# Layer-norm statistics of a diffusion block: full-width TensorE sums, or four narrow products side by side

## The chip, the cores and the metric

The kernel runs on one core of one Trainium2 chip. The metric is device time in microseconds (us) of one execution; lower is better. A core has a matrix engine (TensorE, PE in the profile, with its weight loads as PEld), three engines for elementwise work (VectorE or DVE, ScalarE or ACT, GpSimd or POOL) and queues for transfers. SBUF is the on-chip memory that holds tiles of 128 partitions. PSUM is the memory into which TensorE writes; its banks hold 512 float32 columns on each partition. A matmul with stationary weights of K x M and a moving tile of K x N gives M partitions by N columns, and its time goes by N.

## The reference

Two layers of a hybrid block work on 512 latent tokens and 256 context tokens of width 1024. Each layer is half FFN, token mixing, half FFN, and behind each of the three stands a layer-norm over the 1024 features of a token:

```
def layernorm(x, g, b):
    mu = jnp.mean(xf, axis=-1, keepdims=True)
    var = jnp.mean(jnp.square(xf - mu), axis=-1, keepdims=True)
    return ((xf - mu) * lax.rsqrt(var + LN_EPS) * g + b)

def half_ffn(x, shift, scale, gate, w_in, w_out, g, b):
    h = modulate(x, shift, scale)              # x * (1 + scale) + shift
    a, u = jnp.split(h @ w_in, 2, axis=-1)
    y = (jax.nn.silu(a) * u) @ w_out
    return layernorm(ALPHA * x + 0.5 * gate * y, g, b)
```

The mixers are a Hyena and a gated recurrence in layer 0 and a latent attention in layer 1. The context is carried through layer 0 and the first half FFN of layer 1 only; the output is the latent stream.

## The kernel before

**Layout.** X holds the residual stream with features on partitions: X[128, chunk, token], eight chunks (KC) of 128 features and 768 tokens (TOK), the 512 latents (LAT) first and then the 256 of context (CTX). A layer-norm thus has to add over partitions and over the eight chunks. The program numbers its layer-norms ln0 to ln4 and "final". ln0 to ln3 are worked in two parts: a=0 the context, a=1 the latents. ln4 and final have only latents, in two halves of 256.

**Large products.** Every float32 product of weights and activations is split into high and low parts in the format fp32r, and made of three products: high by high, high by low, low by high (the three lines of `product`, 2914 to 2916, and of `columns`, 2960 to 2962). HHI and HLO are the high and low part of the modulated activations h; GHIA, GLOA, GHIB, GLOB those of the gated ones; WHI*, WLO* those of the weights.

**The statistics.** GpSimd adds some chunks of X into RSTD ahead of TensorE (`add_chunks`, line 844; the table X_ADDED says how many chunks are folded: 7 of the context, 4 of the latents). TensorE then adds what is left over chunks and partitions: `sums` (line 2925) multiplies by ONES, a 128x128 matrix of ones, in plain float32, so that each of the 128 output partitions holds the same sum. ScalarE scales it to the mean MU (line 1292), VectorE subtracts it from X (`center`, line 1842), ScalarE squares (line 1297, tiles SQ), TensorE adds the squares in the same way (`variance`, line 2936), ScalarE takes the root into RSTD (line 1302), VectorE the reciprocal of the whole tile (`inverse`, line 1848) and multiplies (`norm`, line 1855). Mean and root thus stand in SBUF on all partitions, 256 or 512 columns wide. Behind `norm`, ScalarE makes h and its high part (lines 1054, 1057) and VectorE its low part (`low`, line 1825), chunk by chunk; TensorE waits for each chunk of it (semaphore h_lo).

**What sets the order.** Each engine has one hand-written instruction stream, held together by counting semaphores; nothing is scheduled by a planner. TensorE works strictly in its order. Around a layer-norm of two parts it runs: the down products of the context, eight down products of the latents of which the first is followed by the context's sums and the fifth by its variance, then the latents' sums; then `first_pair`, the first products of the next layer: context columns of output half 0 of the slots A and B, the latents' variance, context columns of half 1, and the latent columns. While TensorE makes the context columns of half 1, the latents' root, reciprocal and norm go on beside it. The down product of a chunk of 512 latents is six products of 512 columns; a step k of context columns is three products of 256 columns for each slot. VectorE adds each down product to X (`last_chunk`, line 2272, "eviction" below). ln1 is spread in the same way over the output products of the even mixer, ln4 over those of the odd mixer; in final, the second half's sums and both variances follow the last down product, and then the transposes for the output (line 3659).

**An existing form with narrow weights.** The products of the conditioning vectors (`ada_products`, line 2821) use 32 stationary columns each, four products side by side into the four strips of 32 output partitions.

Of the kernel before, what the change touches and what calls it, by code (L numbers as in the profile page):

```python
# [17 lines left out]
P = 128  # L18
D = 1024
# [9 lines left out]
X_ADDED = {1: 7, 0: 4}  # L29
# [118 lines left out]
def build(nc, A, out):  # L148
# [32 lines left out]
    MU = sb("MU", [P, TOK])  # L181
# [132 lines left out]
    for t, name in ((WQH, "WQH1"), (WQL, "WQL1")):  # L314
# [40 lines left out]
    ln_add, ln_sum, ln_var, ln_mu, ln_cen, ln_sq, ln_std, ln_rstd, ln_n, ln_h32, ln_x = (  # L355
        sem(f"ln_{n}") for n in ("add", "sum", "var", "mu", "cen", "sq", "std", "rstd", "n", "h32", "x"))
# [228 lines left out]
    STAT_BANKS = {"ln0": (3, 4), "ln1": (7, 6), "ln2": (3, 4), "ln3": (3, 4), "ln4": (6, 7), "final": (0, 1)}  # L585
# [6 lines left out]
    def stat_bank(name, a):  # L592
        _, n, s = part(name, a)
        return PS[STAT_BANKS[name][a if name in HALVED else s]][:, 0:n]

# [403 lines left out]
    def _(act):  # L999
# [286 lines left out]
        def layernorm(name, S, j, nxt):  # L1286
            p = plan[name]

            def mean(a):
                lo, n, _ = part(name, a)  # L1290
# [8 lines left out]
            def root(a):  # L1299
                lo, n, _ = part(name, a)  # L1300
                act.wait_ge(ln_var, p.ln + a + 1)
                act.activation(RSTD[:, lo:lo + n], stat_bank(name, a), ACT.Sqrt, bias=EPS[:, 0:1],
                               scale=1.0 / D).then_inc(ln_std, 1)

            if name == "final":
# [5 lines left out]
                mean(1)  # L1311
                for m in range(KC):
                    if m == KC // 2:
                        root(0)
                    square(1, m)
# [362 lines left out]
    def _(dve):  # L1678
# [158 lines left out]
        def center(name, S, a, m):  # L1837

            lo, n, _ = part(name, a)
            if m == 0:  # L1840
                dve.wait_ge(ln_mu, plan[name].ln + a + 1)
            dve.tensor_tensor(X[:, m, lo:lo + n], X[:, m, lo:lo + n], MU[:, lo:lo + n], ALU.subtract).then_inc(ln_cen, 1)

        def inverse(name, S, a):

            lo, n, _ = part(name, a)
            dve.wait_ge(ln_std, plan[name].ln + a + 1)
            dve.reciprocal(RSTD[:, lo:lo + n], RSTD[:, lo:lo + n]).then_inc(ln_rstd, 1)
            dve.wait_ge(ln_rstd, plan[name].ln + a + 1)
            dve.wait_ge(ln_sq, KC * (plan[name].ln + a + 1))  # L1850

        def norm(name, S, a, m):

            lo, n, _ = part(name, a)
            dve.tensor_tensor(X[:, m, lo:lo + n], X[:, m, lo:lo + n], RSTD[:, lo:lo + n], ALU.mult).then_inc(ln_n, 1)
# [36 lines left out]
        def ffn(name, S, j, ada, t0, then, nxt, tables=None):  # L1892
# [86 lines left out]
            if S == 1:  # L1979
# [6 lines left out]
                for m in range(KC):  # L1986
                    center(then, 1, 0, m)
                    if m + 3 < KC:
                        half_chunk(1, m + 3)
                for m in range(KC):  # L1990
# [800 lines left out]
        for a in range(2):  # L2791
            inverse("final", 1, a)
            lo, n, _ = part("final", a)
# [895 lines left out]
```

## Time and profile before

| | |
|---|---|
| time, three runs | 2953.30, 2946.63, 2952.29 us; median 2952.29 us |
| span of the profiled execution | 2945.3 us |
| PE busy | 2859.7 us, 97% of the span, 16175 products |
| PEld busy | 2469.8 us, 84% |
| DVE busy | 2030.9 us, 69% |
| ACT busy | 1049.0 us, 36% |
| POOL busy | 295.6 us, 10% |
| PE waiting in `first_pair` for the low part of h (L2960 <- DVE HLO L1825) | 8.6 us in 5 waits, the longest 4.3 us |
| PE waiting for GpSimd's pre-added chunks (L2925 <- POOL RSTD L844) | 3.3 us in 3 waits |

The span is the time from the first to the last instruction in the profiled execution; the median of the three timed runs is 7.0 us above it, which is what lies around the span and how far a run differs from another. In the profile, a product in plain float32 leaves two records, since it makes two passes; an fp32r product leaves one. Products overlap their neighbours, so what a product costs is read from the distance between starts, not from its own duration. The granted clock (PEclk) is 9 tenths or more in all forty slices of the page, but it can fall in short stretches. In this span ln0 lies at about 645 to 705 us, ln1 at 985 to 1045, ln2 at 1578 to 1640, ln3 at 2119 to 2185, ln4 at 2505 to 2577 and final at 2895 to 2945.

### The profile page before, as it was taken

The numbers are of one execution on the slowest core, as the hardware profiler recorded it, in microseconds if no ns is written. First come the engines' busy times: TensorE is split into PE (matmuls) and PEld (weight loads), VectorE is DVE, ScalarE is ACT, GpSimd is POOL, SyncE is SP. The second block draws the span as 40 slices with busy tenths as digits, with TensorE's granted clock in tenths as the row PEclk, the third lists the DMA queues.
The fourth block names the chain that finished last, engine by engine and source line by source line (L and its number), as shares of the span: only waits on it lengthen the run. The fifth ranks groups of instructions, "written<-read, shape, count | busy, mean of one in ns | idle before, by whom it ended". The sixth has DMA issues, their size and how long they took to land.

```text
span 2945.3 us, 44152 instructions
## 1 busy us (share of the span) xinstructions
PE 2859.7 (97%) x16175; PEld 2469.8 (84%) x16175; DVE 2030.9 (69%) x3254; ACT 1049.0 (36%) x1651; POOL 295.6 (10%) x403
## 2 busy tenths in 40 slices
PE   6999999999999999999999999999999999999998
PEld 2688999987875878998988899999877998878887
DVE  4467767776767477677776887777776887654545
ACT  1422223325650342232323433333255665422123
POOL 1000000011100100101001000000103654100000
PEclk9999999999999999999999999999999999999999
DMA  7434432221213233534432122222310101233331
GB/s 287 147 132 150 144 126 65 64 72 46 61 59 114 86 100 118 174 123 161 129 95 58 43 65 74 69 71 64 88 48 20 29 21 44 58 115 100 100 100 43
DMA packets 301696, 269.64 MB, mean 92 GB/s; under 512 B 31175, under 2 KB 257327, under 8 KB 301456
## 3 DMA queue, kind: packets, MB, share of 16 engines
q1 hardware_dynamic: 278960, 188.95, 21.7%
q0 software_dynamic: 21760, 76.03, 7.3%
q10 hardware_dynamic: 864, 3.15, 0.3%
q8 instruction: 72, 1.18, 0.2%
q14 instruction: 40, 0.33, 0.0%
HBM read 262.85 MB, written 5.24 MB: 91 GB/s over the span
## 4 chain that ended last, share of the span: by engine, by line
PE 88%; DVE 6%; DMA 2%; ACT 2%; issue 1%; POOL 1%; SPq 0%; POOLq 0%; DVEq 0%; ACTq 0%
PE PSALL L2914 14%; PE PSALL L2915 14%; PE PSALL L2916 14%; PE PSALL L3169 8%; PE PSALL L3170 8%; PE PSALL L3171 8%; PE PSALL L2821 2%; PE PSALL L2936 2%; PE PSALL L2960 2%; PE PSALL L2961 2%; PE PSALL L2962 2%; PE PSALL L3592 1%; PE PSALL L3577 1%; PE PSALL L2863 1%; DMA RAW<-in_ffn_w_in_dram 1%
## 5 line engine op out<-in xcount | busy, mean ns | idle before, releaser
L2048 DVE SCALAR_TENSOR_TENSOR X<-PSALL,GATE,X 128x512 f32<-128x512 f32 x480 | 279.5, 611 | 99.7 <-PE PSALL L2916 99.1
L3169 PE MATMUL PSALL<-HHI,WSH 128*128 128x384 f32 x816 | 274.1, 336 | 5.8 <-DVE HLO L2246 5.8
L3170 PE MATMUL PSALL<-HLO,WSH 128*128 128x384 f32 x816 | 274.2, 336 | 0.0
L3171 PE MATMUL PSALL<-HHI,WSL 128*128 128x384 f32 x816 | 273.5, 335 | 0.0
L2914 PE MATMUL PSALL<-GHIA,WHIW 128*128 128x512 f32 (+1 forms) x618 | 217.2, 351 | 13.2 <-DVE X L2048 10.2
L2915 PE MATMUL PSALL<-GLOA,WHIW 128*128 128x512 f32 (+1 forms) x618 | 212.9, 344 | 0.0
L2916 PE MATMUL PSALL<-GHIA,WLOW 128*128 128x512 f32 (+1 forms) x618 | 212.3, 344 | 0.0
L2916 PE MATMUL PSALL<-GHIB,WLOW 128*128 128x512 f32 (+1 forms) x618 | 212.2, 343 | 0.0
L2915 PE MATMUL PSALL<-GLOB,WHIW 128*128 128x512 f32 (+1 forms) x618 | 212.1, 343 | 0.0
L2914 PE MATMUL PSALL<-GHIB,WHIW 128*128 128x512 f32 (+1 forms) x618 | 212.0, 343 | 0.0
L1174 ACT ACTIVATE WSH<-RAW 128x512 fp32r<-128x512 f32 x204 | 129.0, 632 | 223.0 <-DVE RAW L2125 151.3
L3169 PE MATMUL PSALL<-TH,WSH 128*128 128x384 f32 x612 | 206.6, 338 | 0.0
L3171 PE MATMUL PSALL<-TH,WSL 128*128 128x384 f32 x612 | 205.2, 335 | 0.0
L3170 PE MATMUL PSALL<-TL,WSH 128*128 128x384 f32 x612 | 204.7, 334 | 0.0
L2914 PE MATMUL PSALL<-HHI,WHIA 128*128 128x512 f32 (+1 forms) x464 | 168.8, 364 | 1.5 <-DVE WLOA L1724 1.5
L2916 PE MATMUL PSALL<-HHI,WLOA 128*128 128x512 f32 (+1 forms) x464 | 165.3, 356 | 0.0
L2915 PE MATMUL PSALL<-HLO,WHIA 128*128 128x512 f32 (+1 forms) x464 | 165.3, 356 | 0.0
L1065 ACT ACTIVATE WHIW<-RAW 128x1024 fp32r<-128x1024 f32 x96 | 100.0, 1054 | 178.5 <-PE PSALL L2916 97.5
L3169 PEld LDWEIGHTS PSALL<-HHI,WSH 128*128 128x128 f32 x816 | 154.0, 189 | 6.7 <-issue 6.7
L828 POOL DMA_DIRECT2D ADA<-in_ada_w_dram x144 | 76.1, 529 | 824.8 <-PE PSALL L2821 734.0
L2914 PE MATMUL PSALL<-HHI,WHIB 128*128 128x512 f32 (+1 forms) x432 | 157.5, 365 | 1.3 <-DVE MOD L1714 1.3
L844 POOL TENSOR_TENSOR RSTD<-X 128x256 f32<-128x256 f32 (+1 forms) x12 | 14.2, 1184 | 1416.6 <-DVE X L2272 871.2
(411 smaller groups left out, 7329.0 us busy)
## 6 DMA issues: line engine op xcount, KB each, us to landing
RAW<-in_ffn_w_in_dram SPq DMA_DIRECT2D x176, 512.0 KB, 4.1
ADA<-in_ada_w_dram POOLq DMA_DIRECT2D x144, 512.0 KB, 5.6
RAW<-in_ffn_w_out_dram SPq DMA_DIRECT2D x88, 512.0 KB, 3.9
RAW<-in_ev_w_in_dram SPq DMA_DIRECT2D x20, 512.0 KB, 4.0
WRAW<-in_mla_w_q_up_dram SPq DMA_DIRECT2D x16, 288.0 KB, 3.0
RAW<-in_ev_w_out_dram SPq DMA_DIRECT2D x8, 512.0 KB, 4.5
RAW<-in_mla_w_in_dram SPq DMA_DIRECT2D x8, 512.0 KB, 4.3
RAW<-in_mla_w_out_dram SPq DMA_DIRECT2D x8, 512.0 KB, 3.8
```

Source lines behind the costliest of these rows:

```text
L828: pool.dma_start(ADA[slot][:, :], src).then_inc(ada_in[slot], 16)
L1065: act.activation(WHI[slot][:, 1024 * half:1024 * half + 1024], RAW[raw_slot(q)][:, :], ACT.Copy).then_inc(hi_done, 1)
L1174: return act.activation(WSH[:, place, :], raw[:, 512 * cols:512 * cols + 512], ACT.Copy)
L2048: dve.scalar_tensor_tensor(X[:, m, lo:lo + n], down_bank(m, s, 2), GATE[:, j, m, s:s + 1], X[:, m, lo:lo + n], ALU.mult, ALU.add).then_inc ...
L2821: x = te.matmul(PS[3][32 * j:32 * j + 32, 0:D // 4], SC[:, k, :], ADA[slot][:, j * D // 4:(j + 1) * D // 4], start=(k == 0), stop=(k == KC ...
L2914: te.matmul(out, w_hi, x_hi(k), start=(k == 0), stop=False)
L2915: te.matmul(out, w_hi, x_lo(k), start=False, stop=False)
L2916: x = te.matmul(out, w_lo, x_hi(k), start=False, stop=(k == ks - 1))
L2936: x = te.matmul(stat_bank(name, a), ONES[:, :], squares_at(name, a, m), start=(m == 0), stop=(m == KC - 1))
L3169: te.matmul(out, w_hi, hi[block](k), start=(k == 0), stop=False)
L3170: te.matmul(out, w_hi, low[block](k), start=False, stop=False)
L3171: x = te.matmul(out, w_lo, hi[block](k), start=False, stop=(k == 3))
```

## The change

The sums and the squares of a layer-norm are no longer made by one product with 128 columns of ones. `column_sums` makes four products with 32 columns of ones, each on a quarter of the tokens, into the four strips of 32 partitions of one bank. The result is compact: 64 columns (of 256 tokens) or 128 columns (of 512), and the token's quarter is its strip. Mean (MUC), root and reciprocal (RSC) are taken on these compact tiles. `spread` then brings them to all partitions: four products, each with one column of the identity, repeated over 128 weight columns, as weights, and the compact tile as moving data; they write a full-width PSUM bank, from which `center`, `norm` and the last scaling of final now read their second operand, in place of MU and RSTD in SBUF. TensorE has a mean spread and a root spread for each of the twelve parts, with new waits (ln_mu and ln_rstd), and VectorE waits for the spreads (ln_mean, ln_root). GpSimd folds 5 chunks of the context, no longer 7, and TensorE two more.

The pieces are placed anew. In the down products of the latents, the mean is spread after chunk 1, the context's variance comes after chunk 5 instead of 4, and the root is spread after chunk 6. In `first_pair` the latent mean is spread between steps 0 and 1 of the context columns of half 0, the latents' variance lies in four pieces of two chunks each behind steps 0 to 3 of half 1, and the root is spread behind all columns of half 1. ln1, ln4 and final have their own places, as in the diff. ScalarE takes final's first root ahead of the second half's squares, and VectorE its reciprocal between the two centrings.

By count, 28 products of 256 columns and 20 of 512 in `sums`, and 64 and 32 in `variance`, become 100 groups of four products of 64 columns and 52 groups of four of 128; added are 24 spreads of four products, 16 of them 64 columns wide and 8 of 128. The groups stand in 39 separate runs between products of the ordinary form.

```diff
-X_ADDED = {1: 7, 0: 4}
+X_ADDED = {1: 5, 0: 4}
...
-    STAT_BANKS = {"ln0": (3, 4), "ln1": (7, 6), "ln2": (3, 4), "ln3": (3, 4), "ln4": (6, 7), "final": (0, 1)}
+    SUM_BANKS = {"ln0": (4, 6), "ln1": (6, 6), "ln2": (4, 6), "ln3": (4, 6), "ln4": (6, 6), "final": (3, 1)}
+    WIDE_BANKS = {"ln0": (3, 7), "ln1": (7, 3), "ln2": (3, 7), "ln3": (3, 7), "ln4": (7, 5), "final": (4, 0)}
...
-                act.activation(MU[:, lo:lo + n], stat_bank(name, a), ACT.Copy, scale=1.0 / D).then_inc(ln_mu, 1)
+                act.activation(compact(MUC, name, a), sum_bank(name, a), ACT.Copy, scale=1.0 / D).then_inc(ln_mu, 1)
...
-                act.activation(RSTD[:, lo:lo + n], stat_bank(name, a), ACT.Sqrt, bias=EPS[:, 0:1],
+                act.activation(compact(RSC, name, a), sum_bank(name, a), ACT.Sqrt, bias=EPS[:, 0:1],
...
-                dve.wait_ge(ln_mu, plan[name].ln + a + 1)
-            dve.tensor_tensor(X[:, m, lo:lo + n], X[:, m, lo:lo + n], MU[:, lo:lo + n], ALU.subtract).then_inc(ln_cen, 1)
+                dve.wait_ge(ln_mean, plan[name].ln + a + 1)
+            dve.tensor_tensor(X[:, m, lo:lo + n], X[:, m, lo:lo + n], wide_bank(name, a), ALU.subtract).then_inc(ln_cen, 1)
...
-            dve.reciprocal(RSTD[:, lo:lo + n], RSTD[:, lo:lo + n]).then_inc(ln_rstd, 1)
+            dve.reciprocal(compact(RSC, name, a), compact(RSC, name, a)).then_inc(ln_rstd, 1)
...
+            if m == 0:
+                dve.wait_ge(ln_root, plan[name].ln + a + 1)
+                dve.wait_ge(ln_sq, KC * (plan[name].ln + a + 1))
+            dve.tensor_tensor(X[:, m, lo:lo + n], X[:, m, lo:lo + n], wide_bank(name, a), ALU.mult).then_inc(ln_n, 1)
...
+        def column_sums(name, a, m, src):
+            w = quarter(name, a)
+            for q in range(4):
+                x = te.matmul(sum_bank(name, a)[32 * q:32 * q + 32, :], ONES[:, 0:32], src[:, w * q:w * q + w],
+                              start=(m == 0), stop=(m == KC - 1))
+            return x
+        def spread(name, a, t):
+            w = quarter(name, a)
+            for q in range(4):
+                x = te.matmul(wide_bank(name, a)[:, w * q:w * q + w], ID[:, 32 * q:32 * q + 1].broadcast_to([P, P]),
+                              compact(t, name, a), start=True, stop=True)
+            return x
...
-                columns(0, [(slot, 0) for slot in "AB"])
-                variance(ln, 2, 1)
-                columns(0, [(slot, 1) for slot in "AB" if halves[slot] > 1])
+                columns(0, [(slot, 0) for slot in "AB"], lambda k: mean_out(ln, 1) if k == 0 else None)
+                columns(0, [(slot, 1) for slot in "AB" if halves[slot] > 1],
+                        lambda k: variance(ln, 2, 1, (2 * k, 2 * k + 1)) if k < 4 else None)
+                root_out(ln, 1)
...
                     sums(then, 1, 1, lambda m: e0 + KC + m + 1)
+                    variance(then, 1, 0)
+                    mean_out(then, 1)
+                    root_out(then, 0)
+                    variance(then, 1, 1)
+                    root_out(then, 1)
...
                     if m == 0:
                         sums(then, 2, 0, lambda m: e0 + m + 1)
-                    if m == 4:
+                    if m == 1:
+                        mean_out(then, 0)
+                    if m == 5:
                         variance(then, 2, 0)
+                    if m == 6:
+                        root_out(then, 0)
...
-            unit_product("ev_out", "W", p.q + 6, 0, 0, order).then_inc(pe["W"], 1)
+            unit_product("ev_out", "W", p.q + 6, 0, 0, order, after=lambda k: root_out("ln1", 0) if k == 3 else None).then_inc(pe["W"], 1)
...
             chunk(4, 1, between=lambda: sums("ln4", 2, 0, evicted(0)))
+            mean_out("ln4", 0)
...
-            chunk(7, 1)
+            chunk(7, 1, between=lambda: root_out("ln4", 0))
```

**Place 1: TensorE, down products of the latents ahead of ln2, from the end of chunk 0 to the start of chunk 2.** RSTD holds GpSimd's sum of chunks, evac counts evictions. Before:

```order
L2925 MATMUL PSALL<-RSTD,ONES 128x256 [waits ln_add]
L2925 MATMUL PSALL<-X,ONES 128x256 [waits evac]
L2914 MATMUL PSALL<-GHIA,WHIW 128x512
L2915 MATMUL PSALL<-GLOA,WHIW 128x512
L2916 MATMUL PSALL<-GHIA,WLOW 128x512
L2914 MATMUL PSALL<-GHIB,WHIW 128x512
L2915 MATMUL PSALL<-GLOB,WHIW 128x512
L2916 MATMUL PSALL<-GHIB,WLOW 128x512
L2914 MATMUL PSALL<-GHIA,WHIW 128x512 [waits evac]
```

After:

```order
L2950 MATMUL PSALL<-X,ONES 32x64 [waits evac]
L2950 MATMUL PSALL<-X,ONES 32x64 x3
L2929 MATMUL PSALL<-GHIA,WHIW 128x512
L2930 MATMUL PSALL<-GLOA,WHIW 128x512
L2931 MATMUL PSALL<-GHIA,WLOW 128x512
L2929 MATMUL PSALL<-GHIB,WHIW 128x512
L2930 MATMUL PSALL<-GLOB,WHIW 128x512
L2931 MATMUL PSALL<-GHIB,WLOW 128x512
L2958 MATMUL PSALL<-MUC,ID 128x64 [waits ln_mu]
L2958 MATMUL PSALL<-MUC,ID 128x64 x3
L2929 MATMUL PSALL<-GHIA,WHIW 128x512 [waits evac]
```

Two full products of the sums have become four groups of four narrow ones (the last of them is shown), and the spread of the mean, with its wait for ScalarE, stands behind chunk 1.

**Place 2: TensorE, `first_pair` of ln3, where the context columns pass from half 0 to half 1.** SQ are the latents' squares; slot B has one output half of 64 columns here, slot A has two of 128. Before:

```order
L2961 MATMUL PSALL<-HLO,WHIB 64x256
L2962 MATMUL PSALL<-HHI,WLOB 64x256
L2936 MATMUL PSALL<-SQ,ONES 128x512 [waits ln_sq,ln_mu]
L2936 MATMUL PSALL<-SQ,ONES 128x512 [waits ln_sq] x7
L2960 MATMUL PSALL<-HHI,WHIA 128x256 [waits lo_done,h_lo]
L2961 MATMUL PSALL<-HLO,WHIA 128x256
L2962 MATMUL PSALL<-HHI,WLOA 128x256
L2960 MATMUL PSALL<-HHI,WHIA 128x256 [waits h_lo]
```

After:

```order
L3005 MATMUL PSALL<-HHI,WLOB 64x256
L3003 MATMUL PSALL<-HHI,WHIA 128x256 [waits lo_done,h_lo]
L3004 MATMUL PSALL<-HLO,WHIA 128x256
L3005 MATMUL PSALL<-HHI,WLOA 128x256
L2950 MATMUL PSALL<-SQ,ONES 32x128 [waits ln_sq]
L2950 MATMUL PSALL<-SQ,ONES 32x128 x3
L2950 MATMUL PSALL<-SQ,ONES 32x128 [waits ln_sq]
L2950 MATMUL PSALL<-SQ,ONES 32x128 x3
L3003 MATMUL PSALL<-HHI,WHIA 128x256 [waits h_lo]
L3004 MATMUL PSALL<-HLO,WHIA 128x256
```

The variance, one block of eight full products ahead of half 1, is now cut into four pieces inside it.

**Place 3: TensorE, `first_pair` of ln3, where the context columns end and the latent columns (512 wide) begin.** RSC is the compact reciprocal root. After:

```order
L3003 MATMUL PSALL<-HHI,WHIA 128x256 [waits h_lo]
L3004 MATMUL PSALL<-HLO,WHIA 128x256
L3005 MATMUL PSALL<-HHI,WLOA 128x256
L2958 MATMUL PSALL<-RSC,ID 128x128 [waits ln_rstd]
L2958 MATMUL PSALL<-RSC,ID 128x128 x3
L3003 MATMUL PSALL<-HHI,WHIA 128x512 [waits h_lo]
```

Before, the three rows of the last context step were followed at once by the latent columns; now the spread of the root, with its wait for VectorE's reciprocal, stands between them. In ln0, ln2 and ln4 it stands at the same place.

## Rows read from the trace of the kernel before

**Rows 1.** Groups by form, TensorE, line 2936: busy us, mean ns | idle.

```profile
L2936 PE MATMUL PSALL<-SQ,ONES 128*128 128x256 f32 x128 | 28.8, 379 | 0.0
L2936 PE MATMUL PSALL<-SQ,ONES 128*128 128x512 f32 x64 | 28.1, 592 | 0.0
```

**Rows 2.** Timeline, TensorE: start us, us, operation, xcount [idle before <-releaser].

```profile
1071.91 0.39 PE L2916 MATMUL PSALL<-HHI,WLOA 128*128 128x512 f32 x1
1072.23 1.93 PE L2821 MATMUL PSALL<-ADA,SC 128*32 128x256 f32 x32
...
1074.32 0.28 PE L2915 MATMUL PSALL<-HLO,WHIA 128*128 128x256 f32 x1
```

**Rows 3.** Timeline, TensorE, first products of line 2821.

```profile
36.53 0.42 PE L2821 MATMUL PSALL<-ADA,SC 128*32 128x256 f32 x4 [0.98 <-issue]
```

**Rows 4.** Timeline, TensorE, products of 128 columns in the up projections.

```profile
1566.31 0.27 PE L3132 MATMUL PSALL<-TL,WHIB 128*128 128x128 f32 x1
1566.42 0.28 PE L3133 MATMUL PSALL<-TH,WLOB 128*128 128x128 f32 x1
```

**Rows 5.** Groups by form, VectorE (out<-in as partitions x elements) and ScalarE.

```profile
L1848 DVE RECIPROCAL RSTD<-RSTD 128x256 f32<-128x256 f32 x8 | 14.0, 1748 | 5.5 <-ACT RSTD L1302 5.5
L1848 DVE RECIPROCAL RSTD<-RSTD 128x512 f32<-128x512 f32 x4 | 13.4, 3353 | 25.2 <-ACT RSTD L1302 25.2
L1302 ACT ACTIVATE RSTD<-PSALL,EPS 128x512 f32<-128x512 f32 x4 | 2.8, 689 | 19.6 <-PE PSALL L2936 19.6
```

**Rows 6.** Timeline, VectorE and GpSimd, centring of ln2's context.

```profile
1589.09 2.52 DVE L1842 TENSOR_TENSOR X<-X,MU 128x256 f32<-128x256 f32 x4
...
1589.25 1.40 POOL L844 TENSOR_TENSOR RSTD<-X 128x512 f32<-128x512 f32 x1 [3.81 <-DVE X L2272]
```

**Rows 7.** Timeline, ln2, TensorE and VectorE.

```profile
1585.50 0.70 PE L2925 MATMUL PSALL<-RSTD,ONES 128*128 128x256 f32 x2 [1.09 <-POOL RSTD L844]
...
1598.63 1.09 DVE L1855 TENSOR_TENSOR X<-X,RSTD 128x256 f32<-128x256 f32 x3
...
1603.67 0.68 PE L2960 MATMUL PSALL<-HHI,WHIA 128*128 128x256 f32 x1
...
1620.99 1.29 DVE L1855 TENSOR_TENSOR X<-X,RSTD 128x512 f32<-128x512 f32 x2
...
1623.97 0.50 PE L2960 MATMUL PSALL<-HHI,WHIA 128*128 128x512 f32 x1 [1.39 <-DVE HLO L1825]
```

**Rows 8.** Timeline, ln3: last eviction, first context column, first latent column.

```profile
2144.47 0.74 DVE L2272 SCALAR_TENSOR_TENSOR X<-PSALL,GATE,X 128x512 f32<-128x512 f32 x1
...
2146.30 0.68 PE L2960 MATMUL PSALL<-HHI,WHIA 128*128 128x256 f32 x1
...
2166.48 0.80 PE L2960 MATMUL PSALL<-HHI,WHIA 128*128 128x512 f32 x1 [4.26 <-DVE HLO L1825]
```

**Rows 9.** Windows behind three TensorE waits: us, PE busy (x), PEclk, DMA share, GB/s.

```profile
1711.60:1715.00 3.40, 3.40 (x13) 0.50 0.02 5
2166.50:2172.40 5.90, 5.90 (x14) 0.50 0.00 0
2596.30:2599.00 2.70, 2.70 (x12) 1.00 0.59 194
```

**Rows 10.** Timeline, ln4: second mean and norm, and a TensorE wait after it.

```profile
2549.63 0.37 ACT L1292 ACTIVATE MU<-PSALL 128x256 f32<-128x256 f32 x1
...
2560.09 0.76 DVE L1855 TENSOR_TENSOR X<-X,RSTD 128x256 f32<-128x256 f32 x2
...
2576.94 0.50 PE L2914 MATMUL PSALL<-HHI,WHIA 128*128 128x512 f32 x1 [1.48 <-DVE WLOA L1724]
```

**Rows 11.** Timeline, VectorE, final layer-norm, second half of the tokens.

```profile
2934.14 3.25 DVE L2796 SCALAR_TENSOR_TENSOR X<-X,VECS,RSTD 128x256 f32<-128x256 f32 x8
```

**Rows 12.** Timeline, TensorE, products behind its other long waits.

```profile
1710.15 0.41 PE L3169 MATMUL PSALL<-HHI,WSH 128*128 128x384 f32 x1 [3.31 <-DVE HLO L2246]
...
2596.30 0.50 PE L2914 MATMUL PSALL<-GHIA,WHIW 128*128 128x512 f32 x1 [2.59 <-DVE X L1927]
```

More of the change, by code:

```diff
@@ L354, in build @@
     evac = sem("evac")
-    ln_add, ln_sum, ln_var, ln_mu, ln_cen, ln_sq, ln_std, ln_rstd, ln_n, ln_h32, ln_x = (
-        sem(f"ln_{n}") for n in ("add", "sum", "var", "mu", "cen", "sq", "std", "rstd", "n", "h32", "x"))
+    ln_add, ln_sum, ln_var, ln_mu, ln_mean, ln_cen, ln_sq, ln_std, ln_rstd, ln_root, ln_n, ln_h32, ln_x = (
+        sem(f"ln_{n}") for n in ("add", "sum", "var", "mu", "mean", "cen", "sq", "std", "rstd", "root", "n", "h32", "x"))
     flt_in, tab_in, kf_out = sem("flt_in"), sem("tab_in"), [sem(f"kf_out{n}") for n in range(2)]
@@ L1311, in layernorm @@
                 mean(1)
+                root(0)
                 for m in range(KC):
-                    if m == KC // 2:
-                        root(0)
                     square(1, m)
@@ L1989, in ffn @@
                         half_chunk(1, m + 3)
+                inverse(then, 1, 0)
                 for m in range(KC):
@@ L2946, in first_pair, with columns @@
                            for t in (WHI, WLO)]
-            def columns(a, outs):
+            def columns(a, outs, after=None):
                 lo, n, s = part(ln, a)
@@ L2952, in columns @@
                 for k in range(KC):
+                    if after and k:
+                        after(k - 1)
                     te.wait_ge(h_lo, h + KC * a + k + 1)
@@ L3282, in wide, with unit_product @@
                     sums(then, 2, 0, lambda m: e0 + m + 1)
-                if m == 4:
+                if m == 1:
+                    mean_out(then, 0)
+                if m == 5:
                     variance(then, 2, 0)
+                if m == 6:
+                    root_out(then, 0)
             sums(then, 2, 1, lambda m: e0 + KC + m + 1)
-        def unit_product(name, slot, lo_at, half, s, order, wait=None, heads=None):
+        def unit_product(name, slot, lo_at, half, s, order, wait=None, heads=None, after=None):
             lo, width = SEGS[s]
@@ L3298, in unit_product @@
                            lambda k: moving(0, order[k]), lambda k: moving(1, order[k]),
-                           (lambda k: wait(order[k], s)) if wait else None)
+                           (lambda k: wait(order[k], s)) if wait else (lambda k: after(k - 1)) if after else None)
         def gates(n, s):
@@ L3651, in _ @@
         ffn("ffn3", 1, 0, "ln4", "final")
-        variance("final", 1, 0)
-        variance("final", 1, 1)
         for e, (t, half) in enumerate(FIN_TILES):
```

52 lines of the change are left out of this document (32 added, 20 removed).

## The prediction

> **What bounds the kernel now.** I read the page first. TensorE is busy for 97% of the span (the table above). So two things can move the time: less work on TensorE, and the stretches in which it waits for another engine. Next the groups by form: a float32 product with 128 columns of ones costs 28.8/64 = 0.45 us at 256 columns and 28.1/32 = 0.88 us at 512, both passes counted [rows 1]. The 28 + 64 products of 256 and 20 + 32 of 512 are thus 41.4 + 45.8 = 87 us of TensorE. Then the timeline of each layer-norm: TensorE waits 1.09 us for GpSimd ahead of ln2's context sums and 1.39 us for the low part of h ahead of its latent columns [rows 7], 4.26 us at that place in ln3 [rows 8]. ln0 has ln2's shape. Last the clock: behind the 4.26 us wait the granted clock was 0.50, that is 1.2 GHz, for the next 5.9 us [rows 9].
>
> **What the new operations cost.** No row shows a 32-wide product of 64 or 128 columns, so I go by the nearest.
> - *Side by side.* Line 2821 makes 16 products of 256 columns in 1.93 us from first start to last end [rows 2], where one alone takes 0.45; four run at once. A group of four then costs a quarter of a full product: 0.11 us (64 columns each) or 0.22 (128). From above: if every pass costs what it costs in line 2821, 1.72/32 = 0.054 us, a group of eight passes costs 0.43 whatever its width.
> - *Entering and leaving the form.* From 1071.91 to 1074.32 is 2.41 us [rows 2]. In it lie one product of 512 (half of 5.9/14, so 0.21, [rows 9]), sixteen of line 2821 (four groups of 0.43) and one of 256 (0.12). About 0.35 is left for both changes of form. With 39 runs that is 13.7 us.
> - *A spread.* Its weights are 128 columns wide, and with such weights two products of 128 columns start 0.11 us apart [rows 4]. Four products of two passes make 8 x 0.11 = 0.88 us, and 0.17 until the last has landed. From below 0.45 (256 columns at full rate), from above double, 1.8, should loading a repeated column be slower.
> - *VectorE, ScalarE.* The reciprocal takes 1.75 us at 256 and 3.35 at 512 columns [rows 5], 0.0063 a column and 0.14 fixed: 0.54 at 64, 0.95 at 128. A root of 512 takes 0.69 [rows 5]; for 128 I take 0.35. An eviction that reads PSUM lasts 0.74 at 512 columns [rows 8], norm's two from SBUF 1.29, with the last one's tail [rows 7]: a PSUM operand costs between nothing and 0.1 a chunk; I take nothing.
> - *Contention.* Four centrings of 256 took 2.52 us while GpSimd added a chunk [rows 6]; three norms of the same form take 1.09 alone [rows 7], so four take 1.43. 1.1 us went to GpSimd. Centre now has a PSUM operand, and I expect the loss gone; if not, the context's norm comes 1.1 later.
>
> In TensorE work: 100 x 0.11 + 52 x 0.22 = 22, switches 14, spreads 24 x 0.88 = 21, together 57 against 87: 30 us less. But most of what goes stood where VectorE and ScalarE needed the time, so I follow each stage.
>
> The Trainium skill, TensorEngine Tiling (Array Packing), Key Properties, says that changing the tiling mode drains TensorE. The trace agrees, with the 0.35 us above; without a drain the result would be better by up to 14 us.
>
> **ln2, and ln0 like it: 1.7 us each.** Context: with fewer chunks folded the GpSimd wait of 1.09 goes. Sums: 4 groups 0.43 + 0.35; the mean spread is 1.05; the variance 0.86 + 0.35 for 3.6. The context's root comes one down chunk later, VectorE's reciprocal is 1.2 shorter and contention 1.1 less, but the root must pass TensorE behind chunk 6 (0.88 and two handovers). Norm starts at about 1597.7 where it was 1598.63. The last eviction, which the latents' sums need, moves with it, and the last sum behind it takes 0.22, not 0.88: the first context column comes at about 1602.5 instead of 1603.67. From there to the first latent column it took 20.3 us (1623.97). Now: 96 products of 0.12 = 11.5; mean spread 1.05; four variance pieces of 2 x 0.22 + 0.35 = 3.1; root and reciprocal 1.6, covered by the four steps (2.9) behind the last piece; root spread 1.05; then norm, h, its high and its low part, 1620.99 to 1623.97 = 3.0 before and nothing beside it now. Sum 19.7. Gain 0.6 + 1.1.
>
> **ln3: 4.9 us and 2.7 us of clock.** The context's norm comes 1.2 earlier by the same steps, so the last eviction ends at about 1 us before 2145.2 and the first context column is at 2144.3, not 2146.30 [rows 8]: 2.0. From there it took 20.2. Now 72 x 0.12 = 8.6, mean 1.05, pieces 3.1, root and reciprocal 1.6 of which 1.1 are covered, root spread 1.05, then 3.0: 17.3. Gain 2.9. The stretch at half clock held 14 products in 5.9 us [rows 9], which at 0.23 are 3.2: 2.7 more, if the clock stays.
>
> **ln1: 0.7 us.** Its context is bound by VectorE and ScalarE; only the shorter latent reciprocal shows, less the spread.
>
> **ln4: 3.8 us lost.** The latent mean of the second half is made on ScalarE behind five chunks of h, at 2549.63 [rows 10]. The spread of it stands on TensorE behind the first step of columns, queued ahead of seven steps that did not need it. They start at about 2550.4 instead of 2547.4. From there 7 x 0.72, half 1's 8 x 0.72, four pieces of 2 x 0.11 + 0.35 and the root spread, which now stands behind all of half 1: 2550.4 + 5.0 + 5.8 + 2.3 + 0.9 = 2564.4, less up to 0.5 for ScalarE's shorter root and mean ahead of it. Norm was at 2560.09, with half 1 beside it. VectorE's chain behind it is tight up to WLOA, for which TensorE already waits at 2576.94, so the loss passes through.
>
> **final: 2.0 us.** The second scaling starts at 2934.14 [rows 11] and sets the end. Variances of 8 groups cost 1.2, not 3.6, and the two reciprocals 1.2 less each; the second half's mean and root spreads and the root's handovers take back 3. I get about 2932.1.
>
> **Clock.** In ln0, ln2, ln3 and ln4 nothing covers norm and h behind the root spread, so TensorE waits about 3.1 us. Two other waits of before were 3.31 us, ended by the product at 1710.15, and 2.59, ended at 2596.30 [rows 12]; the granted clock was 0.50 from 1711.6 behind the first and 1.00 behind the second [rows 9]. 3.1 lies between. A half clock costs some 1.4 us, half of what ln3 paid for its longer wait. I charge two of four: 2.8.
>
> **Sum.** 1.7 + 1.7 + 0.7 + 4.9 + 2.7 - 3.8 + 2.0 - 2.8 = 7.1 us. On the profiled span that is 2945.3 - 7.1 = 2938.2; with the 7.0 us by which the median exceeds the span, 2945.2 us.
>
> **Rivals.**
> - *Full saving (0.08).* TensorE is the bound to the end, 97% busy, and 26 to 30 us less of its work come through: 2927 at best, or 2935 where only ln4's loss and the clock fail to appear. Against it: at each latent norm the chain through VectorE is what counts.
> - *Given back (0.27).* The clock falls behind all four waits and stays down for longer (another 3 to 6 us), or a start has a price of its own. If eight starts take 0.2 us where the columns need 0.11, the 100 groups of 64 columns cost 9 us more, of which about half lies on the path: 2950. The row of four products as one stretch of 0.42 us [rows 3] shows them beside each other, but doesn't show the starts of passes a quarter as long. Either way 2949 to 2953. The Trainium skill, TensorE: Matmul & The Clock Gate, section "Wait — 56ns, not 53.3ns?", puts the least distance of two starts at about 25 ns, whatever the width; by that the eight passes take 0.2 us, and it is this rival's second form. No run here shows it yet.
> - *The loads set the pace (0.20).* A pass of 64 columns is too short to hide the load of its weights. At 0.054 us a pass a group costs 0.43: 100 x 0.32 + 52 x 0.21 = 43 us more, three quarters of it on the path: 2977. With only the spreads at twice the price, 21 us more, some 19 of 24 on the path: 2962. It decides once a group costs 0.06 us more on average, or a spread 1.3 us. For it speaks that products of 128 columns stand 0.11 apart [rows 4], twice what their columns take; against it that line 2821 kept 0.054 a pass with a load for each, and may be faster still.
> - The forecast's own case has 0.45; its own range is 2937 to 2950.
>
> **How the numbers follow.** Changes under 0.2%, 5.9 us, can't be told from none. Faster: 0.08, most of the forecast case (0.38 of 0.45), and a little of the second rival (0.04): 0.50. Same: the other 0.07, and 0.23 of that rival: 0.30. Slower: 0.20. The range 2934 to 2960 leaves out half of the first rival and most of the third.
>
> **What would show it.** In the profile after: groups of L2950 at 0.11 or 0.22 us, a spread (L2958) at 0.9; ln2's first latent column about 20 us behind its first context column; ln3's about 17, with the clock at 1.00 behind it; ln4's second norm 3.8 later against the last context eviction; TensorE waits of 3.1 us ahead of four latent stretches. The prediction is wrong if L2950's groups are dearer than 0.2 us, if a spread takes over 1.3, or if ln4's first columns are not held by the mean's spread.

## The result, and the profile after

The changed kernel is slower: 2958.70 us (median of ten, 2954.01 to 2964.19) against 2952.23 us (median of ten), ratio 1.0026, 95% interval 1.0017 to 1.0035. Forecast were 2945.2 us. The sign was wrong. The measured time lies inside the stated range, 2934 to 2960, but no case of the text that has this mechanism ends there.

The two profiled executions lie apart by more, 15.3 us (spans 2945.3 and 2960.6): that of before was a low one (2946.63 us) and that of after a high one (2962.55). So I don't compare spans but stages. VectorE runs the same 3254 instructions in both kernels, nearly all in the same order; the difference of the start of the same instruction in two profiles, taken ahead of and behind a layer-norm, tells what that stage gained or lost, whatever went on elsewhere. Positive is later than before. In times of before the stages run from 640 to 740, 985 to 1100, 1575 to 1690, 2110 to 2240, 2500 to 2620 and 2895 to 2938 us; another choice of the instruction moves a number by 0.3 us or less, in final by up to 0.5.

| stage | forecast, without the clock | after | second profile of after |
|---|---|---|---|
| ln0 | -1.7 | +0.9 | +0.9 |
| ln1 | -0.7 | +3.4 | +3.3 |
| ln2 | -1.7 | +2.2 | -1.7 |
| ln3 | -7.6 | -5.4 | -5.3 |
| ln4 | +3.8 | +8.6 | +8.2 |
| final | -2.0 | -1.6 | -1.6 |
| sum | -9.9 | +8.1 | +3.8 |
| outside these stages | 0 | +6.8 | +6.2 |

What lies outside comes in a few single jumps of 0.4 to 2.6 us at the program's start, in ada loads and in other half-clock stretches, at other places in each profile.

The new operations first, groups by form of the changed kernel:

```profile
L2950 PE MATMUL PSALL<-SQ,ONES 128*32 128x64 f32 x512 | 11.3, 223 | 0.1
L2950 PE MATMUL PSALL<-SQ,ONES 128*32 128x128 f32 x256 | 10.3, 279 | 0.0
L2958 PE MATMUL PSALL<-MUC,ID 128*128 128x128 f32 x32 | 7.3, 408 | 0.0
L2958 PE MATMUL PSALL<-RSC,ID 128*128 128x128 f32 x32 | 4.3, 278 | 0.0
```

The variances of 64 squares of 256 and 32 of 512 columns took 28.8 and 28.1 us [rows 1]; they take 11.3 and 10.3, changes of form included. And two groups of the same shape, the spreads of four means and of four roots of 512 tokens, differ: 7.3 and 4.3 us. Equal work at unequal cost is a matter of the clock, as the windows below show. The timeline of ln2's context variance, in plain products, shows the unit prices:

```profile
1601.22 0.39 PE L2931 MATMUL PSALL<-GHIB,WLOW 128*128 128x512 f32 x1
1601.54 1.10 PE L2950 MATMUL PSALL<-SQ,ONES 128*32 128x64 f32 x64
1602.57 0.50 PE L2929 MATMUL PSALL<-GHIA,WHIW 128*128 128x512 f32 x1
1602.90 0.40 PE L2930 MATMUL PSALL<-GLOA,WHIW 128*128 128x512 f32 x1
```

The sixty-four passes (two of each product) start within 0.88 us, 14 ns apart on average: eight groups of 0.11. Another 0.15 pass until the next ordinary product starts. With 0.09 more than usual at the entrance and 0.10 more behind, a change in and out costs 0.34. The forecast had 0.11 and 0.35. VectorE's part:

```profile
L1866 DVE TENSOR_TENSOR X<-X,PSALL 128x512 f32<-128x512 f32 x32 | 21.5, 681 | 9.0 <-PE PSALL L2958 9.0
L1858 DVE RECIPROCAL RSC<-RSC 128x64 f32<-128x64 f32 x8 | 4.4, 546 | 9.7 <-ACT RSC L1314 9.7
L1858 DVE RECIPROCAL RSC<-RSC 128x128 f32<-128x128 f32 x4 | 3.8, 954 | 24.1 <-ACT RSC L1314 24.1
```

Reciprocals of 0.55 and 0.95, as in the sum, for 1.75 and 3.35 [rows 5]. The contention is gone too: beside a GpSimd add of 1.29 us, four centrings with a PSUM operand take 1.41, where they took 2.52 [rows 6]:

```profile
1598.11 1.41 DVE L1853 TENSOR_TENSOR X<-X,PSALL 128x256 f32<-128x256 f32 x4
1598.27 1.29 POOL L858 TENSOR_TENSOR RSTD<-X 128x512 f32<-128x512 f32 x1 [5.93 <-DVE X L2284]
```

So every operation is as cheap as it was priced. Now TensorE in ln2, in the changed kernel's timeline, where [rows 7] had two waits:

```profile
1605.39 1.10 PE L2958 MATMUL PSALL<-RSC,ID 128*128 128x64 f32 x8 [1.17 <-DVE RSC L1858]
...
1609.66 0.43 PE L2950 MATMUL PSALL<-X,ONES 128*32 128x128 f32 x8 [0.90 <-DVE X L2284]
1610.99 0.66 PE L2950 MATMUL PSALL<-X,ONES 128*32 128x128 f32 x8 [0.90 <-DVE X L2284]
1613.02 1.74 PE L2958 MATMUL PSALL<-MUC,ID 128*128 128x128 f32 x8
...
1628.42 1.05 PE L2958 MATMUL PSALL<-RSC,ID 128*128 128x128 f32 x8
1632.48 0.79 PE L3003 MATMUL PSALL<-HHI,WHIA 128*128 128x512 f32 x1 [3.02 <-DVE HLO L1836]
```

Before, full products of 0.88 us filled the time until VectorE had evicted the next chunk; the groups of 0.22 don't, and TensorE waits 1.17, 0.90 and 0.90 us within seven microseconds. Behind that the mean's spread takes 1.74 us where the root's takes 1.05. And the latent columns begin behind a wait of 3.02. ln0 is like it; in ln3 the sums have only the two waits of 0.90, the first of them here:

```profile
2154.54 0.42 PE L2950 MATMUL PSALL<-X,ONES 128*32 128x128 f32 x8 [0.90 <-DVE X L2284]
```

The windows of the changed kernel in ln2 (us, PE busy (x), PEclk, DMA share, GB/s) name the cause:

```profile
1609.00:1611.00 2.00, 0.44 (x10) 1.00 0.00 0
1611.00:1614.40 3.40, 3.40 (x21) 0.50 0.00 0
1613.00:1614.50 1.50, 1.50 (x10) 0.52 0.00 0
1614.40:1616.40 2.00, 2.00 (x19) 0.99 0.01 4
1631.50:1638.30 6.80, 5.82 (x14) 0.50 0.00 0
1632.45:1638.50 6.05, 6.02 (x15) 0.51 0.00 0
```

The granted clock is half at both places, 1.2 GHz. The run before had one such stretch in ln0 to ln4 [rows 9]; this one has twelve, each 3.4 or 6.8 us long, 51 us together: in each of the five layer-norms at its first columns (behind the thin sums) and at its latent columns (behind the wait for h), and two more about ln4.

The other runs say the same. Each has its mean granted clock on record: a run at 0.985 over 2957 us spent 0.030 of them, 89 us, at half clock. By this it is 90 us on average in the ten runs of the change (77 to 101), 55 us in the 29 runs of before that stand beside the first experiments. Over all 132 runs on record, compared with runs of the same kernel in the same series, each further microsecond of half clock goes with 0.33 us more time. The 35 us more are then some 12 us, an estimate, against the 6.5 us by which the change is slower.

### The profile page after: what moved, and what is told of

The parts are those of the page before. It is cut to its first block, busy times and chain, and to the rows that moved or that the text cites. A ratio compares the mean times of both kernels' runs of the same rounds, so it can differ in the third digit from the quotient of the medians.

```text
span 2960.6 us, 46366 instructions
## 1 busy us (share of the span) xinstructions
PE 2857.2 (97%) x17295; PEld 2481.4 (84%) x17295; DVE 2009.5 (68%) x3254; ACT 1043.2 (35%) x1651; POOL 287.4 (10%) x395
## 3 DMA queue, kind: packets, MB, share of 16 engines
q8 instruction: 81, 1.33, 0.2%
## 4 chain that ended last, share of the span: by engine, by line
PE 88%; DVE 6%; DMA 2%; ACT 1%; issue 1%; SPq 0%; POOL 0%; DVEq 0%; ACTq 0%; POOLq 0%
PE PSALL L2929 14%; PE PSALL L2930 14%; PE PSALL L2931 14%; PE PSALL L3224 8%; PE PSALL L3225 8%; PE PSALL L3226 8%; PE PSALL L3003 2%; PE PSALL L3005 2%; PE PSALL L3004 2%; PE PSALL L2836 2%; PE PSALL L3652 2%; PE PSALL L3637 1%; PE PSALL L2878 1%; PE PSALL L3517 1%; PE PSALL L2958 1%
## 5 line engine op out<-in xcount | busy, mean ns | idle before, releaser
L2930 PE MATMUL PSALL<-HLO,WHIB 128*128 128x512 f32 (+1 forms) x432 | 154.6, 358 | 0.0
```

The lines of the kernel that those rows point to most:

```text
L2930: te.matmul(out, w_hi, x_lo(k), start=False, stop=False)
```

## The same program twice

The changed kernel was profiled a second time to see whether the stretches belong to their places.

> The changed kernel unchanged, for a second profile of it. If the half-clock stretches belong to the places, the same ten stand at the same places in ln0 to ln4. If they are a matter of chance at places that allow them, some are gone and others have come, and the ledger of ln0 and ln2 moves between -1.7 us (none) and +2 (two or three), 1.75 us for each stretch of 3.5 us.

Measured: 2957.5 us. In ln2 the same waits, to a hundredth, and another clock. (This profile was taken with a later series, perhaps on another chip: which chip made the first one is not on record. But the ten runs of the change in one series differ among themselves by up to 24 us of half clock.) Timeline of TensorE in ln2, second profile:

```profile
1610.40 0.43 PE L2950 MATMUL PSALL<-X,ONES 128*32 128x128 f32 x8 [0.90 <-DVE X L2284]
1611.72 0.43 PE L2950 MATMUL PSALL<-X,ONES 128*32 128x128 f32 x8 [0.90 <-DVE X L2284]
1612.89 1.05 PE L2958 MATMUL PSALL<-MUC,ID 128*128 128x128 f32 x8
...
1631.66 0.50 PE L3003 MATMUL PSALL<-HHI,WHIA 128*128 128x512 f32 x1 [3.01 <-DVE HLO L1836]
```

and its windows:

```profile
1612.80:1614.00 1.20, 1.20 (x13) 1.00 0.00 0
1632.35:1638.50 6.15, 6.15 (x28) 1.00 0.00 0
```

In 6.1 us behind the wait it starts 28 products, the first profile 15. ln2 comes out at -1.7 us, the forecast's own number for it without a fall; with 10.2 us of half clock it was +2.2. That is 3.9/10.2, or 0.38 us lost for each microsecond of half clock (it would be 0.50 if TensorE had work all through; part lies in waits), near the 0.33 of the runs. ln0, ln1 and ln3 kept their stretches; in ln4 there are again four, but one stands elsewhere and one is only half as long. The second profile has ten, 38 us together. The first latent column of ln2 follows the first context column by 19.6 us here, where the forecast had 19.7. The expectation named "ten"; I had not counted two of ln4's. The Trainium skill, TensorE: Matmul & The Clock Gate, section "What's actually happening", says of a kernel's first products that the point at which the clock changes differs from run to run of one kernel; here that is so in the middle of a kernel, with 3.9 us between the two profiles in one stage.

## The experiments

### Filling the waits ahead of the latent columns

```diff
                 root_out(ln, 1)
+                for i in range(12):
+                    te.matmul(PS[6][:, 0:P], ONES[:, :], ID[:, :], start=True, stop=True)
```

> The changed kernel with twelve extra float32 products of 128 columns (about 0.22 us each at full clock, so 2.6 us) behind the root spread of ln0 to ln4, in the wait of 2.5 to 3.2 us ahead of the latent columns; their result is used by nothing. Clock theory (the idle waits pull the granted clock to 0.50 for the first 3 to 4 us of the latent columns): the clock stays at 1.00 behind the filler, the columns start when they did, and each of the five places gains 1.2 to 2.4 us, 7 to 9 us in all, so about 2950. Order theory (the loss is the wait itself, the clock is a side effect): the columns start no earlier, the time is within 2 us of the changed kernel's 2958.7. Price theory (the new small products are dearer than they look): 13 us of more products, later by up to that.

Measured: 2953.20 us, ratio to before 1.0006 (0.9996 to 1.0017), 5.5 us faster than the change. None of the five latent stretches is at half clock any more, where without filling 27 of 35 were (five layer-norms in each of the seven profiles that have the root spread in its place of the change); those at the first columns remain in ln1, ln3 and ln4. ln0 and ln2 stand at -1.7, ln1 at +0.7. The columns start no earlier: what comes of it comes by the clock. TensorE's timeline in ln2 shows 0.34 us of wait left of 3.02:

```profile
1632.39 0.50 PE L3003 MATMUL PSALL<-HHI,WHIA 128*128 128x512 f32 x1 [0.34 <-DVE HLO L1836]
1632.73 0.40 PE L3004 MATMUL PSALL<-HLO,WHIA 128*128 128x512 f32 x1
```

It brought 5.5 where 7 to 9 were expected. The mean half clock of its runs is 70 us, 20 fewer than the change has, and at 0.33 that is 6.6. That ln0 and ln2 lost the stretches at their first columns too, where nothing was filled, is chance.

### Filling the gaps in the latents' sums

```diff
             for m in [0] + list(range(count + 1, KC)) if ms is None else ms:
+                if a == 1 and m >= 6 and name in ("ln0", "ln2", "ln3"):
+                    for i in range(3):
+                        te.matmul(PS[4][:, CTX:CTX + P], ONES[:, :], ID[:, :], start=True, stop=True)
                 te.wait_ge(*((ln_add, done + count) if m == 0 else (evac, evicted(m))))
```

> The changed kernel with three extra float32 products of 128 columns (0.22 us each) ahead of each of the last two groups of the latents' sums in ln0, ln2 and ln3, where TensorE waits 0.9 us twice for evictions; their result is used by nothing. Clock theory (TensorE, thinly used around the narrow sums, falls to half clock for the next 3 us): the clock stays at 1.00 at the first context columns and the mean spread, each of the three gains 1.0 to 1.5 us, 2955. If what the chip sees is the narrow products themselves and not the gaps, the clock falls all the same and the time is the changed kernel's, 2958.7 to 2960.

Measured: 2954.34 us, ratio 1.0009 (0.9997 to 1.0021), 4.4 us faster than the change. In ln0, ln2 and ln3, which were filled, no stretch stands at the first columns; in ln1 and ln4, which were not, it does. In the nine profiles in which these gaps are not filled, 15 of 27 first columns of the three layer-norms ran at half clock; in this one and the last one below, where the gaps are filled, none of six. With the narrow products unchanged, it is the gaps between them that let the clock fall. In ln3, which has no wait of 1.17, two of 0.90 us are enough.

### The late mean of ln4

```diff
-                columns(0, [(slot, 0) for slot in "AB"], lambda k: mean_out(ln, 1) if k == 0 else None)
+                columns(0, [(slot, 0) for slot in "AB"], lambda k: mean_out(ln, 1) if k == (4 if ln == "ln4" else 0) else None)
```

> The changed kernel with the spread of ln4's second mean behind step 4 of the context columns, not behind step 0. Order theory: TensorE no longer stands 2.4 us for ScalarE's mean, so ln4's second norm comes 2.4 us earlier. Clock theory: the half-clock stretch behind that wait (6.5 us, 3.2 lost) goes as well, so 5 to 5.6 us in all, 2953.5. If the spread's place does not matter (the squares would hold the variance anyway): no change, 2958.7.

Measured: 2956.93 us (2949.62 to 2965.62), ratio 1.0024 (1.0013 to 1.0035). The median moved by 1.8 us, within what the runs scatter. In the profile ln4 stands at +4.8, not +8.6, but it has 10 us less of half clock there, which has its part in the 3.9. In the changed kernel the spread waited 2.44 us for ScalarE and ran at half clock:

```profile
2557.88 1.97 PE L2958 MATMUL PSALL<-MUC,ID 128*128 128x64 f32 x8 [2.44 <-ACT MUC L1305]
```

in this one there is no wait:

```profile
2550.13 1.00 PE L2958 MATMUL PSALL<-MUC,ID 128*128 128x64 f32 x8
```

To part the two, the distance from ln4's first root spread to its second: 24.01 us in the change with 6.8 us of half clock between, 23.07 in the run with filled waits with 3.4, and 20.10 here with none. That is 0.28 us for a microsecond of half clock, and some 2.0 us for the place of the spread, near the 2.4 expected. In its ln0 and ln2, where nothing was changed, no clock fell, and they stand at -1.7 both: the same chance as above.

### The root spread beside the last steps

```diff
-                columns(0, [(slot, 1) for slot in "AB" if halves[slot] > 1],
-                        lambda k: variance(ln, 2, 1, (2 * k, 2 * k + 1)) if k < 4 else None)
-                root_out(ln, 1)
+                late = 3 if halves["B"] > 1 else 5
+                columns(0, [(slot, 1) for slot in "AB" if halves[slot] > 1],
+                        lambda k: variance(ln, 2, 1) if k == 0 else root_out(ln, 1) if k == late else None)
```

> The changed kernel with the latents' variance in one piece behind step 0 of the context columns of half 1, and the root spread behind step 3 (step 5 in ln3) and not behind all eight. Order theory: norm and h then run beside the last four steps (2.9 us), the wait of about 3 us ahead of the latent columns goes nearly whole in ln0, ln1, ln2 and ln4, a third of it in ln3, and three switches of form fewer give 1 us each: about 3 to 4 us for each of the four and 1.5 in ln3, 14 us, so about 2945; with the clock kept on top another 5, so 2940. Clock theory alone: without the wait the clock stays up, gain 1.5 us a place, 2951. Price theory: 3 us of switches saved, 2956.

Measured: 2935.70 us, ratio 0.9955 (0.9940 to 0.9970), 23.0 us faster than the change and 16.5 faster than before. The forecast of this run, 14 to 19, was too small. TensorE in ln2 has no wait behind the spread:

```profile
1613.81 1.05 PE L2958 MATMUL PSALL<-RSC,ID 128*128 128x128 f32 x8
...
1617.88 0.50 PE L3003 MATMUL PSALL<-HHI,WHIA 128*128 128x512 f32 x1
```

4.07 us from spread to latent columns as in the changed kernel, but now with 24 products of context between them. No clock falls at the latent columns of ln0, ln1, ln2 and ln4. In ln3 the place covers only part, and the clock falls as before:

```profile
2152.32 0.50 PE L3003 MATMUL PSALL<-HHI,WHIA 128*128 128x512 f32 x1 [2.30 <-DVE HLO L1836]
```

and in the window behind it:

```profile
2152.90:2156.30 3.40, 3.40 (x10) 0.50 0.00 0
```

By stage: ln0 -4.0, ln1 -3.0, ln2 -5.6, ln3 -8.5, ln4 +3.5, final -1.6, together -19.1. To part its two edits:

### One variance alone

```diff
                 columns(0, [(slot, 1) for slot in "AB" if halves[slot] > 1],
-                        lambda k: variance(ln, 2, 1, (2 * k, 2 * k + 1)) if k < 4 else None)
+                        lambda k: variance(ln, 2, 1) if k == 0 else None)
                 root_out(ln, 1)
```

> The changed kernel with the latents' variance of ln0 to ln4 in one piece behind step 0 of half 1, the root spread still behind all eight steps. It parts what the early root spread brought (from 2958.7 to 2935.7 us, both edits together). Order theory (the place of the root spread did it): only the three switches saved per layer-norm, 1.0 us each, 5 us in all, about 2953; the wait ahead of the latent columns stays at 2.5 to 3 us. Switch theory (cutting the variance into pieces was the loss): most of the 23 us, so 2940 or less. In ln3 one piece also ends the variance earlier, and the three steps that cover the root and reciprocal become seven: about 1 us more there.

Measured: 2954.10 us, ratio 1.0005 (0.9995 to 1.0015), 4.6 us faster than the change. The mean half clock of its runs is that of the change (90 us), so the clock has no part in it. The switches saved are worth what they were priced at; the other 18 us of the early spread are its place, and the clock that comes with it.

### Seven chunks folded by GpSimd

```diff
-X_ADDED = {1: 5, 0: 4}
+X_ADDED = {1: 7, 0: 4}
```

> The changed kernel with GpSimd folding 7 chunks of the context again, as before, and not 5. If the shorter fold brought what was forecast, undoing it costs the wait for GpSimd (1.25 us ahead of the context sums) in ln0, ln2 and ln3, of which 0.8 to 1.2 reach the first context column: 3 us, about 2962. If VectorE's evictions hold that column anyway (they hold the last sums now): under 1 us, 2958.7 to 2959.5. TensorE makes two groups of four fewer per layer-norm, 0.2 us.

Measured: 2963.92 us, ratio 1.0035 (1.0020 to 1.0051), 5 us slower than the change by medians. ln0 and ln2, each with the same half clock as in the first profile of the change (6.8 and 10.2 us), go from +0.9 to +1.7 and from +2.2 to +3.2. So the shorter fold brings 0.8 to 1.0 us a layer-norm, as expected. The stretches of half clock stand at the same first and latent columns as in the first profile of the change, eleven of them, 55 us in all. The intervals of the two ratios overlap, so the 5 us are no more than a tendency.

### Every spread twice

```diff
-            for q in range(4):
+            for q in list(range(4)) * 2:
                 x = te.matmul(wide_bank(name, a)[:, w * q:w * q + w], ID[:, 32 * q:32 * q + 1].broadcast_to([P, P]),
```

> The changed kernel with the four products of every spread issued twice (the second time over the same result). It prices a spread on the path: at 0.88 us as forecast, 24 of them are 21 us at most, some 19 on the path 17 us, 2975. If the loads of a repeated column did not overlap (the rival that priced a spread at 1.8), 24 x 1.8 = 43 us, 2995 or more. If the spreads lay beside waits that end later anyway: under 8 us.

Measured: 2978.08 us, ratio 1.0079 (1.0057 to 1.0102) to a before of 2954.89 in that series; against the change's 1.0026 that is 0.53%, 15.6 us, 0.65 us for each of 24. In ln0, where no clock fell in this profile, four more spreads moved the stage from -1.7 to +1.9, 0.9 us each. The rest of the kernel had less half clock than the change, 31 us in the stages of this profile, so that the 0.65 is on the low side. The spreads are on the path, and where the clock did not fall they cost the 0.88 of the sum; the rival that a repeated column's load doubles them is out.

### Both places mended

The early root and ln4's late mean together, both diffs from above:

> The root spread behind step 3 (ln3: 5) with the variance in one piece, and ln4's second mean spread behind step 4: both edits together. If they are independent, as the order theory has it: 2935.7 less the 3.9 us that the late mean spread saved in ln4 by the profile, 2932. If the squares, which wait for the centring behind the mean, then hold the variance behind step 0 of half 1: 1 to 2 us of it are given back, 2934.

Measured: 2929.34 us (2928.15 to 2933.06, 4 runs), ratio 0.9925 (0.9904 to 0.9945). Stages: ln0 -4.1, ln1 -2.9, ln2 -4.0, ln3 -8.4, ln4 -0.2, final -1.4, together -21.0; six stretches of half clock are left. And with ln4's first root spread behind chunk 7 and the sums' gaps filled:

```diff
-            chunk(7, 1, between=lambda: root_out("ln4", 0))
+            chunk(7, 1)
+            root_out("ln4", 0)
```

> Root and mean spreads placed as in the run with both edits, and besides ln4's first root spread behind the down product of chunk 7 and not in the middle of it (TensorE stood there 2.8 us for the reciprocal), and the three extra products ahead of each of the latents' last two groups in ln0, ln2 and ln3. Order theory: the rest of chunk 7, 1.4 us, runs in that wait and ln4 gains 1.4. Clock theory: in ln0, ln2 and ln3 no half-clock stretch at the first context columns, another 1 to 1.5 us where there was one. Together 2929. If the clock's falls there are a matter of chance and cost little now: 2931.

Measured: 2930.79 us (4 runs), ratio 0.9922 (0.9899 to 0.9944): the same within the intervals. Its profile stands 24.7 us below before in the six stages, with no stretch of half clock in ln0, ln2 and ln3 (-5.6, -5.5 and -9.7), but with ln4 at +0.3. The moved root did bring its gain: TensorE's wait for the reciprocal there goes from 1.87 us (not the 2.8 of the expectation) to 0.43, and from ln4's first mean spread to its second root spread it takes 27.00 us, not 28.20, with 3.4 us of half clock between in both. A stretch of half clock behind ln4, at 2587.7, took as much again. These two are the fastest versions, 22 and 23 us ahead of the kernel before.

## Why the prediction was wrong

**The step that failed is the clock.** The text charged "two of four: 2.8" us, for the four waits of about 3.1 us. The waits came (3.02 in ln0, ln2 and ln3, and in ln1 too, for which the text had none; 2.05 in ln4). But the clock fell at all five latent places in the first profile, and at all five first columns as well, for which the forecast had no term. The price of one fall was right, 1.4 us for what measures 1.3 (3.4 us at 0.38); their number was not. 51 us of half clock at 0.38 are 19 us, where before had 7 us of it. The sum of the other terms, -9.9, plus 19, is +9 against the +8.1 that the stages show. In the second profile 38 us are 14 us of loss, and +4 against +3.8. The 0.38 comes from one of these stages; with the 0.33 of the runs the sums are +7 and +3. Without the 12 us that the runs' extra half clock costs, the change would be 5.5 us faster, where the forecast had 7.1 with no net cost of the clock in it.

It had two faults. I counted the waits by their length against two examples of before (3.31 fell, 2.59 did not [rows 9, 12]), but ln4's wait of 2.05 us, shorter than the one that did not fall, was followed by half clock in five of seven profiles. And I took each wait by itself; the runs show short ones close together (1.17, 0.90 and 0.90, in ln3 only the last two) doing the same. The second fault: I took narrow sums as time saved without asking what TensorE would do with it: VectorE's evictions, 1.33 us apart, set the pace there, so a sum of 0.22 in place of 0.88 turned into gaps. The rival "given back" came nearest, with the clock in all four places, and priced it at 3 to 6 us more; it had a chance of 0.27 and ended at 2953, and of its 0.27 all but 0.04 was counted as no change. The chance for slower, 0.20, was wholly that of the rival of the loads, which fell. That 2958.70 lies inside the range is luck.

One sum of the text does not come out: under "full saving", 7.1 us with ln4's 3.8 and the clock's 2.8 added back are 13.7, which gives 2938.6 and not 2935. Nothing else rests on it.

**ln0 and ln2, "1.7 us each": right.** Every profile of the change, or of it with a late mean or filled waits, in which no clock fell there shows -1.7 (ln0 twice, ln2 four times).

**ln3, "4.9 us and 2.7 us of clock": right in its first part.** -5.4 with 6.8 us of half clock; -6.8 with 3.4 us in the run with filled sums. Carried on to none, about -8 against the -7.6 of both terms: but the gain of 2.7 for an undisturbed clock was booked and not received, since a new wait stood in place of the old.

**ln1, "0.7": right without the clock**, by the run with filled sums: +1.9 with 6.8 us of half clock, less 2.6. It has the longest wait, 3.2 us for the last eviction where before had 0.79, which I had not named.

**ln4, "3.8 us lost": about right.** The wait for the mean was 2.44 us at 2557.88. Less 0.38 us for each microsecond of half clock, the two profiles of the change leave 2.1 and 3.0 (of +8.6 and +8.2), those with filled waits and filled sums 4.6 and 3.3. The early root and late mean take the stage to -0.2, so the loss was where the spreads stood.

**final, "2.0": 1.6.** **Prices of the new operations**: all held, 0.11 and 0.34, 0.88, 0.55 and 0.95. The rival of the loads (0.20), and the starts' price (its second form, inside the 0.27), fell: passes of 64 columns start 14 ns apart on average. The Trainium skill's least distance of about 25 ns (TensorE: Matmul & The Clock Gate, section "Wait — 56ns, not 53.3ns?") isn't what four products side by side show here.

**The 7.0 us "by which the median exceeds the span"** were mostly that the profiled execution was a low one (2946.63 us, 1.3 above its span). It moved no difference.

**What stays open**: why the same waits of 0.90, 0.90 and 3.0 us end at half clock in one execution and at full in another. The runs show both; none shows what decides. The share of the early root's 18 us that is the clock was not parted from that of the order. Its profile has 34 us of half clock fewer than the first one of the change, some 12 us; its six runs have 20 us fewer on average, some 7 us.

## What to carry to other kernels

Work saved on an engine that waits for others at that point becomes a gap, and on TensorE a gap has a second price: look at what fills the time, not only at what is shorter. A broadcast that must go through TensorE belongs a few steps ahead of the end of independent work, so that the chain behind it (here 3 us of norm, h and its low part) has cover; that place was worth 18 us, with what the clock gave back, where the whole change had been forecast to bring seven. And a stage whose clock can fall should be profiled more than once before it is called a gain or a loss.

## What the runs showed of the hardware

Two waits of 0.90 us, 1.3 us apart, can be followed by 3.4 us of half clock (ln3, six of nine profiles), and need not be. Ahead of the latent columns a wait of 3.0 us was followed by half clock in 22 of 28 places, one of 2.05 in five of seven. The stretches of half clock in these stages were 3.4 or 6.8 us long, and each microsecond of them cost 0.33 to 0.38 us. With plain products whose result nobody reads put in such waits, the clock stayed at 1.00 at all eleven places where they were tried (five waits ahead of latent columns, three in the sums' gaps in each of two kernels). Four 32-wide float32 products side by side keep their quarter price down to 64 columns: 0.11 us for four, where one full product of 256 takes 0.45. To change from the ordinary form to this one and back cost 0.34 us. VectorE operations with one operand from PSUM were not slowed by GpSimd's adds: four took 1.41 us beside an add, where four with both operands in SBUF had taken 2.52.
